# The delta inverse of a hybrid stack on one core: its levels as products of block-diagonal 128x128 matrices

## The reference

```python
decay = jnp.where(causal, jnp.exp(jnp.where(causal, diff, 0.0)), 0.0)
L = jnp.where(strict, jnp.einsum('bhnid,bhnjd->bhnij', k_beta, k) * decay, 0.0)
eye = jnp.eye(C, dtype=f32)
T = lax.linalg.triangular_solve(eye + L, jnp.broadcast_to(eye, L.shape), left_side=True, lower=True, unit_diagonal=True)
u = T @ v_beta
w = T @ (k_beta * jnp.exp(g_cum)[..., None])
qk = jnp.where(causal, jnp.einsum('bhnid,bhnjd->bhnij', q, k) * decay, 0.0)
def step(state, xs):
    qd, kd, u_c, w_c, qk_c, gl = xs
    v_new = u_c - w_c @ state
    o = qd @ state + qk_c @ v_new
    state = state * jnp.exp(gl)[..., None, None] + jnp.einsum('bhck,bhcv->bhkv', kd, v_new)
    return state, o
```

## Time and profile before

| | us |
|---|---|
| median of three runs | 2710.59 (2709.77 to 2711.96) |
| the profiled execution | 2711.97 |
| its span in the profile | 2710.2 |
| the eight heads of the delta stage | 336.6, from 557.86 to 894.42 of the span |
| the first head, the second, one from inside the loop, the last | 39.85, 43.39, 42.59, 40.40 |

### The profile page before, as it was taken

The page is one execution under the profiler, slowest core; times in us unless marked ns, Lnnn a source line. Parts: engine busy times, 40 slices in busy tenths (PEclk is TensorE's granted clock), DMA queues, the critical chain, the costliest instruction groups (busy, mean ns, idle before and its releaser), DMA issues.

```text
span 2710.2 us, 41985 instructions
## 1 busy us (share of the span) xinstructions
PE 2662.8 (98%) x13878; PEld 2135.0 (79%) x13878; DVE 1385.6 (51%) x2452; ACT 1226.7 (45%) x1908; POOL 1076.0 (40%) x803
## 2 busy tenths in 40 slices
PE   8999999999999899999999999999999999999999
PEld 6887777777777677788887888887788877888886
DVE  7435333687778567787755321128753444222126
ACT  5334434455554455565544433235564553333234
POOL 5544333333333342443434544444412213544442
PEclk9999999999999999999999999999999999999999
DMA  4332222212111222222222333332211212333331
GB/s 159 101 101 83 80 70 77 70 55 63 33 60 51 65 71 63 86 78 69 71 70 85 101 95 93 99 109 89 78 39 47 62 31 70 107 95 93 98 103 55
DMA packets 59643, 211.89 MB, mean 78 GB/s; under 512 B 6688, under 2 KB 7072, under 8 KB 59552
## 3 DMA queue, kind: packets, MB, share of 16 engines
q1 hardware_dynamic: 57744, 206.89, 25.5%
q10 hardware_dynamic: 1520, 2.75, 0.3%
q0 software_dynamic: 288, 1.05, 0.1%
HBM read 208.57 MB, written 2.10 MB: 78 GB/s over the span
## 4 chain that ended last, share of the span: by engine, by line
PE 70%; DVE 5%; issue 2%; ACT 2%; POOL 0%; DVEq 0%; POOLq 0%; ACTq 0%
PE bank L1327 18%; PE bank L1329 17%; PE bank L1328 17%; PE bank L3344 2%; PE bank L1455 2%; PE bank L3338 1%; PE bank L424 1%; PE bank L426 1%; PE bank L425 1%; DVE activations_low L454 1%; PE bank L1480 1%; PE bank L2194 1%; PE bank L3329 1%; PE bank L3332 1%; PE bank L3330 1%
## 5 line engine op out<-in xcount | busy, mean ns | idle before, releaser
L374 POOL TENSOR_TENSOR weights_low<-weights_raw,weights_high 128x512 fp32r<-128x512 f32 x776 | 1043.6, 1368 | 1443.1 <-ACT weights_high L358 1418.7
L1327 PE MATMUL bank<-activations_high,weights_high 128*128 128x512 f32 x2912 | 1178.9, 405 | 30.4 <-POOL weights_low L374 14.5
L1329 PE MATMUL bank<-activations_high,weights_low 128*128 128x512 f32 x2912 | 1139.9, 391 | 0.0
L1328 PE MATMUL bank<-activations_low,weights_high 128*128 128x512 f32 x2912 | 1139.8, 391 | 0.0
L1327 PEld LDWEIGHTS bank<-activations_high,weights_high 128*128 128x128 f32 x2912 | 549.4, 189 | 163.3 <-issue 18.8
L1329 PEld LDWEIGHTS bank<-activations_high,weights_low 128*128 128x128 f32 x2912 | 549.2, 189 | 116.8
L1328 PEld LDWEIGHTS bank<-activations_low,weights_high 128*128 128x128 f32 x2912 | 550.0, 189 | 108.9 <-issue 6.7
L358 ACT ACTIVATE weights_high<-weights_raw 128x1024 fp32r<-128x1024 f32 x384 | 403.7, 1053 | 282.0 <-PE bank L1329 275.0
L2975 DVE TENSOR_TENSOR mixed<-bank,mixed 128x512 f32 (+1 forms) x48 | 33.2, 692 | 193.9 <-PE bank L1329 193.9
L2919 ACT ACTIVATE to_split<-work 128x512 f32<-128x512 f32 x64 | 40.5, 632 | 181.5 <-DVE work L2961 181.5
L2961 DVE SCALAR_TENSOR_TENSOR work<-bank,rstd 128x512 f32<-128x512 f32 x64 | 44.2, 690 | 140.2 <-PE bank L1329 134.1
(11 more groups left out here) (471 smaller groups left out, 3314.1 us busy)
## 6 DMA issues: line engine op xcount, KB each, us to landing
weights_raw<-weights SPq DMA_DIRECT2D x388, 512.0 KB, 3.6
out_t<-residual SPq DMA_DIRECT2D x8, 256.0 KB, 2.1
residual<-x_t ACTq DMA_DIRECT2D x2, 512.0 KB, 7.6
residual<-x_t POOLq DMA_DIRECT2D x2, 512.0 KB, 10.1
work<-p_t ACTq DMA_DIRECT2D x2, 512.0 KB, 4.6
const<-consts SPq DMA_DIRECT2D x1, 713.0 KB, 12.8
const<-consts SPq DMA_DIRECT2D x1, 321.0 KB, 11.8
root<-positions ACTq DMA_DIRECT2D x1, 256.0 KB, 3.3
```

Source lines behind the costliest of these rows:

```text
L374: K.nc.gpsimd.tensor_tensor(K.w_lo[:, s, part], K.raw[:, s, part], K.w_hi[:, s, part].bitcast(F32), ALU.subtract).then_inc(K.job_sems["low ...
L1327: K.nc.tensor.matmul(dst, wh, K.act_hi[:, t, :], start=k == 0, stop=False)
L1328: K.nc.tensor.matmul(dst, wh, K.act_lo[:, t, :], start=False, stop=False)
L1329: ins = K.nc.tensor.matmul(dst, wl, K.act_hi[:, t, :], start=False, stop=k == len(tiles) - 1)
```

## The change

The levels work on whole arrays. For the products w1 to w5 and dt1 to dt4 the left operand is now a block-diagonal 128x128 matrix (both chunks of a block, with zeros outside its two diagonal blocks), and the helper both_halves issues four matmuls with 128 rows, 128 columns and 64 moving columns where halves issued eight of 64x64. The masked matrices lie in the buffers of gates and tmp, which are cleared once after the gates are done; s_two, also cleared once, holds s in the same form. dt5, ds5, w6 and ds6 stay as they were, and b.s with them.

DVE no longer copies um's diagonal blocks into umc. It masks straight from um, with one instruction for the top and one for the bottom (level()), and the subtraction from the identity and the transposes of levels 0 to 3 are two instructions each as well. Of the four steps of the value convolution two are issued at the end of the head ahead, behind its normalize; one stays at the head's start, one in level 1, and none is left behind kd. Nine more instructions of DVE in a head report a step (GDN_STEPS).

```diff
+        def both_halves(use, lhs, rhs):
+
+            for c in range(NG):
+                ins = mm(chunk(bank(use), c), lhs[:, c, :], rhs[:, c, :], start=True, stop=True)
+            ring.written(ins)
...
-            halves(f"w{l}", b.um2[l % 2], b.tt)
+            both_halves(f"w{l}", b.um2[l % 2], b.tt)
...
-            halves(f"dt{l}", b.s, b.w)
+            both_halves(f"dt{l}", b.s_two, b.w)
...
-        halves("w5", b.um2[1], b.tt)
+        both_halves("w5", b.um2[1], b.tt)
...
+    def level(l):
+
+        um2 = b.um2[l % 2]
+        st.step(v.tensor_tensor(um2[TOP, :, TOP], b.um[TOP, :, TOP], each(f"level{l}", TOP), ALU.mult))
+        return v.tensor_tensor(um2[BOTTOM, :, BOTTOM], b.um[BOTTOM, :, BOTTOM], each(f"level{l}", BOTTOM), ALU.mult)
...
+    for um2 in b.um2:
+        st.step(v.memset(um2, 0.0))
+    st.wait()
     e.eng.sem_inc(ring.free[0], 1)
     e.eng.sem_inc(K.sem("gdn_o_free"), 1)
     e.eng.sem_inc(K.sem("gdn_begin"), 1)
     e.eng.sem_inc(K.sem("gdn_head"), 1)
     normalize()
+    take(convolutions(0, (2,)), 2)
...
-        conv_v, conv = convolutions(i, (2,)), convolutions(i + 1, (0, 1)) if more else swa_angles(e)
+        conv_v, conv = value_ends(i), convolutions(i + 1, (0, 1)) if more else swa_angles(e)
...
-        st.step(v.tensor_copy(b.umc[TOP], b.um[TOP, :, TOP]))
-        step(v.tensor_copy(b.umc[BOTTOM], b.um[BOTTOM, :, BOTTOM]))
-        step(v.tensor_tensor(b.u0, b.umc, each("level0"), ALU.mult))
-        step(v.tensor_tensor(b.s, each("ident2"), b.u0, ALU.subtract))
-        flat_s, flat_t = (a.rearrange("p a b -> p (a b)") for a in (b.s, b.tt))
-        step(v.transpose(flat_t, flat_s))
-        v.tensor_tensor(b.u1, b.umc, each("level1"), ALU.mult).then_inc(K.sem("gdn_um"), 1)
+        step(level(0))
+        for h in HALVES:
+            st.step(v.tensor_tensor(b.s_two[h, :, h], each("ident2", h), b.um2[0][h, :, h], ALU.subtract))
+        st.wait()
+        for h in HALVES:
+            st.step(v.transpose(b.tt[h], b.s_two[h, :, h]))
+        st.wait()
+        level(1).then_inc(K.sem("gdn_um"), 1)
...
-            v.tensor_tensor(b.um2[(l + 1) % 2], b.umc, each(f"level{l + 1}"), ALU.mult).then_inc(K.sem("gdn_um"), 1)
+            level(l + 1).then_inc(K.sem("gdn_um"), 1)
...
-                take(conv_v, 2)
+                take(conv_v, 1)
...
-            v.transpose(flat_s, flat_t).then_inc(K.sem("gdn_s"), 1)
+            if l < 4:
+                st.step(v.transpose(b.s_two[TOP, :, TOP], b.tt[TOP]))
+                v.transpose(b.s_two[BOTTOM, :, BOTTOM], b.tt[BOTTOM]).then_inc(K.sem("gdn_s"), 1)
...
-                take(conv_v, 1)
...
         if more:
             select(i + 1)
             normalize(i)
+            take(convolutions(i + 1, (2,)), 2)
```

More of the change, by code:

```diff
@@ L1358, in gdn_buffers @@
     b = Names()
-    (b.u, b.t, b.x, b.taps, b.bg, b.eg, b.tok, b.f1, b.hb, b.hg, b.hf, b.egl, b.ea, b.umc, b.u0, b.u1, b.s, b.tt, b.w,
+    (b.u, b.t, b.x, b.taps, b.bg, b.eg, b.tok, b.f1, b.hb, b.hg, b.hf, b.egl, b.ea, two, b.s, b.tt, b.w,
      b.sf, b.qkt, b.nwt, b.vn, b.st) = carve(
         K, (3, 516), (3, S), (3, S), (12,), (S,), (S,), (NG, 64), (NG, H8), (NG,), (NG,), (NG,), (NG,),
-        (2,), (NG, 64), (NG, 64), (NG, 64), (NG, 64), (NG, 64), (NG, 64), (NG, GC), (NG, GC), (S,), (2, P), (2, P))
-    b.um2 = [b.u0, b.u1]
+        (2,), (NG * GC,), (NG, 64), (NG, 64), (NG, 64), (NG, GC), (NG, GC), (S,), (2, P), (2, P))
+    b.u0, b.s_two = b.w, two.rearrange("p (a b) -> p a b", a=NG)
     b.z, b.dt = K.sq[:, 0, :], K.sq[:, 1, :].rearrange("p (a b) -> p a b", a=NG)
@@ L1368, in gdn_buffers @@
     b.qd, b.o, b.r, b.gates, b.tmp = (m[:, k * S:(k + 1) * S] for k in range(3, 8))
+    b.um2 = [by_block(b.gates), by_block(b.tmp)]
     b.row1, b.row2, b.part = K.act_hi[:, 15, :], K.act_lo[:, 15, :], K.act_hi[:, 14, :]
@@ L1794, in gdn_dve @@
     st.step(v.memset(b.sf, 0.0))
+    st.step(v.memset(b.s_two, 0.0))
     st.step(v.tensor_copy(b.ones_r, K.c("ones")[:, 0:P]))
@@ L1813, in across, with each @@
         return a.unsqueeze(2).broadcast_to([P, NG, P])
-    def each(name, parts=slice(0, P)):
+    def each(name, parts):
         return K.c(name)[parts, 0:CH].unsqueeze(1).broadcast_to([parts.stop - parts.start, NG, CH])
+    def level(l):
+        um2 = b.um2[l % 2]
+        st.step(v.tensor_tensor(um2[TOP, :, TOP], b.um[TOP, :, TOP], each(f"level{l}", TOP), ALU.mult))
+        return v.tensor_tensor(um2[BOTTOM, :, BOTTOM], b.um[BOTTOM, :, BOTTOM], each(f"level{l}", BOTTOM), ALU.mult)
     def first_convolution(part):
@@ L1826, in first_convolution, with value_ends @@
             if n < 2:
+                step(ins)
+            else:
+                ins.then_inc(K.sem("gdn_conv"), 1)
+            yield
+    def value_ends(j):
+        u, t = b.u[:, 2, :], b.t[:, 2, :]
+        for n in range(2, 4):
+            ins = v.scalar_tensor_tensor(t, u[:, n:n + S], b.taps[:, 8 + n:9 + n], t, ALU.mult, ALU.add)
+            if n < 3:
                 step(ins)
@@ L1968, in head @@
             ring.wait_read(f"dt{l}", i)
-            v.transpose(flat_s, flat_t).then_inc(K.sem("gdn_s"), 1)
+            if l < 4:
+                st.step(v.transpose(b.s_two[TOP, :, TOP], b.tt[TOP]))
+                v.transpose(b.s_two[BOTTOM, :, BOTTOM], b.tt[BOTTOM]).then_inc(K.sem("gdn_s"), 1)
+            else:
+                v.transpose(b.s.rearrange("p a b -> p (a b)"), b.tt.rearrange("p a b -> p (a b)")) \
+                    .then_inc(K.sem("gdn_s"), 1)
             if l == 1:
@@ L2052, in gdn_dve @@
     swa_angles_dve(e)
-GDN_STEPS = 26
+GDN_STEPS = 35
 TWO_PI_HI = 6.28125
```

## The result

The changed kernel takes 2763.78 us (median of five, 2762.88 to 2770.11), the kernel before 2710.96 beside it (2709.77 to 2712.63): a ratio of 1.0198, 95% interval 1.0187 to 1.0209. It is 53 us slower; the forecast was 17 us slower, with a range that ended at 2739.

The account below looks back on a forecast made before the run. PE's queue was taken as the bound. Heads 1 to 7 add 7 x 2.36 = 16.5 us, head 0 -1.5, the opening +2.2: +17.2 on 2711.97, 2729.2, or 2727.8 as median; range 2700 to 2739.

Parts of the forecast that it names:

- PE, the nine products: Nine small products of a head on PE: full-array passes save 0.22 us each, 2.0 us in a head.
- The upper bound: Dearest price of a new PE product, from passes with 128 moving columns: 0.88 to 0.92 us, 0.9 lost in a head.
- rival 3: Slower by PE itself: passes of 0.11 us, products 0.92 for 0.82, time 2720; chance 0.08.
- DVE up to level 1: DVE from head start to level 1's masks: one of the pair waits for POOL, w1 1.0 us later.
- rival 4: Slower: both of level 1's pair behind POOL, w1 at 651.5, levels 2 and 3 find POOL idle; 2733, chance 0.10.
- The walk: Main forecast, following DVE, POOL and PE through a head's levels: 2.4 us more in a head; chance 0.50, range 2717 to 2739.
- Levels 2 to 5: Later levels in a head: PE waits 0.6 us at w2, 0.7 at w3, 1.8 at w4; w5 2.5 later.
- all four rivals: Alternatives to the main forecast: faster 2697 (0.19), no change 2711 (0.13), rival 3 2720 (0.08), rival 4 2733 (0.10).
- The opening: Ahead of head 0, two memsets and two convolution steps stand before PE's start of the stage: +2.2 us.

Follow-up runs that it names:

- the products over 64 rows: Changed kernel with the nine products over the upper 64 rows only, the lower half of the contraction left out: 2852 us in one run.
- the nine transposes: Kernel before, with the 32x32 transpose ahead of level 1's mask issued nine times in place of once: 2738.66 us.
- the filled wait: Changed kernel with two projection steps more issued ahead of w1 in heads 1 to 7: 2750.47 us, and again 2749.58.
- The move alone: Kernel before, with only two of the four value convolution steps moved ahead of each head: 2715.43 us.
- all causes removed: Changed kernel with one whole mask per level, POOL's output scaling behind the masks, head 0's convolution not ahead, and products tiled 64x64: 2724.17 us.

## Why the prediction was wrong

The direction was right, and in part for the reason given: masks on DVE that stand behind POOL, with PE waiting for them. Of the 36 us that it missed by, these are the steps.

**PE, the nine products: the sign was wrong.** The text took 0.60 us for eight passes from the earlier trace rows, "since those passes have the same weights' width and the same moving width", and saved 2.0 in a head. The passes start 0.112 apart, as those of 128 moving columns do. The head's PE work grew by 1.07 to 1.43: 3.1 to 3.4 us off in each head, some 25 in the stage. The upper bound (0.9 lost) was nearer, and it too was passed. Passes of 0.11 are rival 3's condition, at 0.08. The rule that was weighed against, from the Trainium skill, "TensorE: Matmul & The Clock Gate", section "LDWEIGHTS (loading the stationary operand)", is the columns of the weights divided by 1.2 GHz, whatever the rows: by it 107 ns for 128 columns and 53 for 64, as estimates. The 0.112 with 128 rows, the 0.112 with 64 rows and the 0.058 in each group of 64 columns agree with it. The transposes of the earlier trace rows do start 0.06 apart, and have the very shape of the products over 64 rows, so the rule does not price them; they are a different operation, and I took a price across operations. Why they are faster, no run here shows.

**DVE up to level 1: the mechanism of rival 4, at 0.10.** Rivals 3 and 4 stood as alternatives; both came, and together. The walk had the pair ask at 7.0 us into the head, 0.04 after POOL began, and let "a chance of a few hundredths" decide on the first half. A pair costs 0.87 in place of 0.75 and the transposes 0.91 in place of 0.82; so the pair asks at 7.3. POOL stood where it was said to (6.9), and both halves waited. PE waited 1.96 us ahead of w1. (The row that the text gives for a subtraction from PSUM not waiting, 651.71 in the earlier trace rows, stands beside an idle POOL, whose instruction ended at 651.03; what it says holds all the same, in the changed kernel at 727.21, where the subtraction takes 0.42 under POOL's run.)

**Levels 2 to 5.** The waits for w2 (0.6) and w3 (0.7) did not come, as rival 4 had it: POOL was idle at level 2's pair, and the second half of level 3's started 0.06 before POOL did (721.41 and 721.47), which is luck. The one for w4 did: 0.94, where the walk had 1.8. In a head 2.9 us of new waits came for 4.1 forecast (1.0, 0.6, 0.7, 1.8), and the walk was too dark here: a slower PE has less to wait for.

**The granted clock was no term of the sum.** The prediction named 1.00 in the earlier trace rows and used it throughout. The stretches at 0.5 cost up to 19 us. This step is missing in the walk and in all four rivals, and it is the cause that no row of before prices: no stretch lies in a head there. That long single waits bring it is shown by the nine transposes (stretches without any part of the change) and by the filled wait. That one such wait is not enough is shown as well, by the heads that have it and keep 1.00. What decides between them, and how it adds up over several waits and half-empty passes, is open.

**The opening.** 2.2 us forecast, all ahead of the stage. The move alone cost 4.3 to the time, as a wait of 4.0 inside head 0 and half clock behind it; in the changed kernel the stage starts 1.4 later, the wait is 3.9, and head 0 and the later start make 7.0 together, of which the products and pairs have a part. Between the heads the steps cost nothing, as said.

In sum, by the changed kernel's own rows: 7 x 4.3 = 30 us of longer heads at full clock (10 of PE's work, 20 of waits), 16 for heads 2, 4 and 7 at half clock, 7 for head 0 and the start, 1 for the stretch in head 1, less 2 in the rest of the program: 52, and the two spans differ by 51.9. Against the forecast that is 14 more for the heads at full clock (4.3 for 2.36, seven times), 16 for the clock, 6 for head 0 and the opening (7.0 for 0.7) and 1 for head 1, less the 2. The kernel with all causes removed is at +12.6, so removing them takes back 40 of the 53 us as well. No variant was faster than the kernel before, and none points to one: its PE waits only 0.5 us in a head.

## What to carry to other kernels

Price an operation from a row of the same operation, not only of the same shape; where the only row is of another, keep the next one's price as the likelier. Where an engine with shared access to memory runs at a known time, splitting an instruction in two doubles the waits, and a distance of a few hundredths between the two engines is no distance: take the costlier side. When PE is the bound and a change puts a wait of two microseconds in front of small products, add a term for the clock (5.6 us in heads 2 and 4 of the changed kernel, nothing in heads 3, 5 and 6), and look for a step of other work that can stand in the gap.

## What the runs showed of the hardware

A full-array fp32 pass of 64 moving columns took 0.112 us from start to start, with 128 or with 64 rows of weights; two passes of 64 columns of weights each, in different columns of the array, took 0.058 together (one run). A two-input instruction of 64 partitions behind POOL ended 0.28 to 0.3 us after POOL's (715.38 against 715.09), and each of a pair waited anew. Two instructions of 64 partitions and 256 elements took 0.87 us in place of 0.43 for one of 128x256, with POOL idle: the halves are not served side by side. PE's wait of 2.7 us in front of tiled products brought 3.4 us at half clock in every other loop head; the same waits in two heads of one execution had a clock of 1.00 in one and 0.96 in the other. And half of the array's rows left empty in nine products of a head held the clock at 0.50 for 41 us at a time (one run).
